# Layer 1's causal mask moved from two TensorE products a pass to one VectorE add; layer 0's compressed results in one bank

## The reference

```python
s_own = jnp.einsum('bhqd,bhkd->bhqk', qc, kown)
m_own = (own + jnp.arange(MOBA_BLOCK))[None, :] <= tpos[:, None]
p = masked_softmax(s_own * HEAD_DIM ** -0.5, m_own)      # masked scores are -inf, their probability is 0
o = jnp.einsum('bhqk,bhkd->bhqd', p, vown)
```

## Time and profile before

| | |
|---|---|
| median of 3 runs | 770.12 us (768.23 to 773.03) |
| the profiled execution | 768.51 us, span 766.7 us |
| PE busy | 745.8 us (97%), 5045 matmuls |
| DVE busy | 497.6 us (65%), 682 instructions |
| ACT busy | 380.4 us (50%), 574 instructions |
| DMA | 146.50 MB, 191 GB/s over the span |
| granted TensorE clock | 9 tenths or more in all 40 slices |

### The profile page before, as it was taken

The page is one execution under the profiler, slowest core; times in us unless marked ns, Lnnn a source line. Parts: engine busy times, 40 slices in busy tenths (PEclk is TensorE's granted clock), DMA queues, the critical chain, the costliest instruction groups (busy, mean ns, idle before and its releaser), DMA issues.

```text
span 766.7 us, 12234 instructions
## 1 busy us (share of the span) xinstructions
PE 745.8 (97%) x5045; PEld 640.7 (84%) x5045; DVE 497.6 (65%) x682; ACT 380.4 (50%) x574; POOL 25.6 (3%) x43
## 2 busy tenths in 40 slices
PE   5999998999999999999999999999999999999998
PEld 3677885468888868788999999999878999999886
DVE  1476759647756755885779999747863745545431
ACT  2554566646354656454553354598443544444330
POOL 3100000100000000012000000000000000000000
PEclk9999999999999999999999999999999999999999
DMA  9994546933367353353746555423444554454611
GB/s 368 406 379 143 200 165 248 390 160 138 110 220 274 110 220 138 138 176 110 274 167 218 168 183 201 167 82 115 160 172 157 220 221 171 159 221 167 217 56 55
DMA packets 21958, 146.50 MB, mean 191 GB/s; under 512 B 2588, under 2 KB 2716, under 8 KB 5392
## 3 DMA queue, kind: packets, MB, share of 16 engines
q1 hardware_dynamic: 20880, 142.62, 50.0%
q0 software_dynamic: 752, 2.06, 0.8%
q10 hardware_dynamic: 272, 1.05, 0.3%
HBM read 144.68 MB, written 1.05 MB: 190 GB/s over the span
## 4 chain that ended last, share of the span: by engine, by line
PE 78%; DVE 3%; issue 2%; ACT 1%; POOL 0%; POOLq 0%; DVEq 0%; ACTq 0%
PE banks L455 22%; PE banks L457 22%; PE banks L456 22%; PE banks L543 3%; PE banks L631 2%; DVE WL L1678 1%; PE banks L567 1%; PE banks L670 1%; PE banks L638 1%; PE banks L923 0%; PE banks L599 0%; PE banks L908 0%; PE banks L674 0%; DVE KT L1710 0%; PE banks L664 0%
## 5 line engine op out<-in xcount | busy, mean ns | idle before, releaser
L1678 DVE TENSOR_TENSOR WL<-RAW,WH 128x2048 fp32r<-128x2048 f32 (+1 forms) x104 | 236.0, 2279 | 63.8 <-ACT WH L1170 63.4
L1170 ACT ACTIVATE WH<-RAW 128x2048 fp32r<-128x2048 f32 (+1 forms) x104 | 197.6, 1906 | 79.0 <-PE banks L457 65.7
L455 PE MATMUL banks<-HH,WH 128*128 128x256 f32 x768 | 217.9, 284 | 0.0
L456 PE MATMUL banks<-HL,WH 128*128 128x256 f32 x768 | 217.3, 283 | 0.0
L457 PE MATMUL banks<-HH,WL 128*128 128x256 f32 x768 | 217.3, 283 | 0.0
L456 PEld LDWEIGHTS banks<-HL,WH 128*128 128x128 f32 x768 | 147.4, 192 | 0.1
L455 PEld LDWEIGHTS banks<-HH,WH 128*128 128x128 f32 x768 | 147.3, 192 | 0.1
L457 PEld LDWEIGHTS banks<-HH,WL 128*128 128x128 f32 x768 | 147.3, 192 | 0.0
L455 PE MATMUL banks<-WH,HH 128*128 128x512 f32 (+1 forms) x320 | 127.1, 397 | 3.5 <-DVE HL L1737 1.9
L457 PE MATMUL banks<-WH,HL 128*128 128x512 f32 (+1 forms) x320 | 124.3, 389 | 0.0
L456 PE MATMUL banks<-WL,HH 128*128 128x512 f32 (+1 forms) x320 | 124.1, 388 | 0.0
(11 more groups left out here) (292 smaller groups left out, 906.1 us busy)
## 6 DMA issues: line engine op xcount, KB each, us to landing
RAW<-in_weights_dram SPq DMA_DIRECT2D x114, 1024.0 KB, 4.8
BIG<-in_weights_dram SPq DMA_DIRECT2D x6, 1024.0 KB, 4.9
ROTS<-in_weights_dram SPq DMA_DIRECT2D x4, 1024.0 KB, 7.0
PROBS<-in_weights_dram SPq DMA_DIRECT2D x2, 1024.0 KB, 12.0
RAW<-in_weights_dram SPq DMA_DIRECT2D x2, 816.0 KB, 9.9
GATE<-in_weights_dram SPq DMA_DIRECT2D x3, 512.0 KB, 9.9
X<-in_x_dram ACTq DMA_DIRECT2D x1, 1024.0 KB, 6.2
QT<-in_weights_dram SPq DMA_DIRECT2D x1, 1024.0 KB, 13.7
```

The costliest lines, as they stand in the source:

```text
L455: pe.matmul(out_, lhsT=w[0], rhs=x[0], start=start, stop=False, **more)
L456: pe.matmul(out_, lhsT=w[0], rhs=x[1], start=False, stop=False, **more)
L1170: do(act.activation(WH[:, home[n], 0:kb * width], RAW[:, slot[n] % RAW_RING, 0:kb * width], ACT.Copy), high_done)
L1678: do(dve.tensor_tensor(WL[:, home[n], w], RAW[:, slot[n] % RAW_RING, w], WH[:, home[n], w], ALU.subtract), low_done)
```

## The change

TensorE leaves the two mask products out in layer 1 (`by_vector`: every pass from layer 1's first), and the last score product marks the bank full. VectorE's `peaks` then adds the mask to the two diagonal blocks of both heads, in place in the two score banks, and waits for that before its minima. In layer 0, kc2 and vc2 go to one bank, columns 0 to 29 and 128 to 255, opened and drained once. The turns of qb (and of q1_1 in layer 1) take "out" banks. The compressed scores are issued at the end of step 3, behind the turns of the probabilities (`last`), and the conditioning row of step 4 behind the weighing (`after`). On VectorE `lows(13)` moves from step 3, ahead of the compressed mask, to the head of step 4's list; on ScalarE the eviction of cmpT moves ahead of `highs(16)` and the gate of zb.1.

On TensorE:

```diff
+        def by_vector(p):
+            return p >= spans[1][0]
...
-            def head_turn(name, t):
+            def head_turn(name, t, kind="turn"):
                 i = rot_index[(name, t)]
-                turn(f"{name}.{t}.T", [QR[:, i % 2, j * P:(j + 1) * P] for j in range(4)], [(roped, i + 1)])
+                turn(f"{name}.{t}.T", [QR[:, i % 2, j * P:(j + 1) * P] for j in range(4)], [(roped, i + 1)], kind)
...
-                        pe.matmul(out_, lhsT=half_of(q, QT, q // 2, t * P, (t + 1) * P),
-                                  rhs=half_of(q, KT, kb, 0, (t + 1) * P), start=(t == 0), stop=False)
+                        mm = pe.matmul(out_, lhsT=half_of(q, QT, q // 2, t * P, (t + 1) * P),
+                                       rhs=half_of(q, KT, kb, 0, (t + 1) * P), start=(t == 0), stop=(by_vector(p) and t == 1))
+                        if by_vector(p) and t == 1:
+                            ps.fill(mm, f"s.{u}")
+                if by_vector(p):
+                    return
...
-            def attention(layer, extra, after={}):
+            def attention(layer, extra, after={}, last={}):
...
                         probs_turn(i - 1)
+                    for what in last.get(i - a, ()):
+                        what()
...
-                ps.fill(mm, "kc2")
                 pe.wait_ge(hid_done, 3)
-                bank = ps.open(pe, "proj", "vc2")
                 for g in range(2):
                     for hb in range(2):
-                        mm = pe.matmul(bank[:, g * HD:(g + 1) * HD],
+                        mm = pe.matmul(bank[:, P + g * HD:P + (g + 1) * HD],
...
-                ps.fill(mm, "vc2")
+                ps.fill(mm, "kc2")
...
-                ps.wait_drained(pe, "vc2")
                 turn("cmpT", [CP[:, t, 4 * g:4 * g + 4, :].rearrange("p h c -> p (h c)")
...
-            attention(0, {0: [lambda: by_tokens("qb", 0), lambda: by_features("za", 0)], 1: [lambda: by_tokens("qb", 1), lambda: head_turn("qb", 0)],
-                          2: [lambda: by_features("za", 1), lambda: head_turn("qb", 1), compress_out],
-                          3: [lambda: by_features("zb", 0)], 4: [lambda: conditioning_row(0, 4)],
+            attention(0, {0: [lambda: by_tokens("qb", 0), lambda: by_features("za", 0)], 1: [lambda: by_tokens("qb", 1), lambda: head_turn("qb", 0, "out")],
+                          2: [lambda: by_features("za", 1), lambda: head_turn("qb", 1, "out"), compress_out],
+                          3: [lambda: by_features("zb", 0)],
...
-                      {3: [compressed_scores]})
+                      {4: [lambda: conditioning_row(0, 4)]}, {3: [compressed_scores]})
...
-                          1: [lambda: head_turn("q1_1", 0), lambda: by_tokens("k1_1", 0),
-                              lambda: head_turn("q1_1", 1)],
+                          1: [lambda: head_turn("q1_1", 0, "out"), lambda: by_tokens("k1_1", 0),
+                              lambda: head_turn("q1_1", 1, "out")],
```

On ScalarE:

```diff
-                evict("kc2", KCT[:, :, :], lambda bank: bank[:, 0:2 * NC].rearrange("p (g c) -> p g c", g=2))
-                evict("vc2", VCM[:, :, :], lambda bank: bank[:, 0:P].rearrange("p (g d) -> p g d", g=2))
+                bank = ps.wait_filled(act, "kc2")
+                do(act.activation(KCT[:, :, :], bank[:, 0:2 * NC].rearrange("p (g c) -> p g c", g=2), ACT.Copy))
+                ps.drain(act.activation(VCM[:, :, :], bank[:, P:2 * P].rearrange("p (g d) -> p g d", g=2), ACT.Copy), "kc2")
...
-                          5: [lambda: highs(16), lambda: gate_half("zb.1", 3), lambda: evict("cmpT", CPT[:, :, :], flat2)],
+                          5: [lambda: evict("cmpT", CPT[:, :, :], flat2), lambda: highs(16), lambda: gate_half("zb.1", 3)],
```

On VectorE, in `peaks` and in layer 0's list:

```diff
+                if by_vector(p):
+                    diagonal = both_scores[:, :, 0:TRI].rearrange("p u (b c) -> p u b c", b=3)[:, :, 0:3:2, :]
+                    mask = const("maskw")[:, 0:P].unsqueeze(1).unsqueeze(1).to_broadcast([P, 2, 2, P])
+                    do(dve.tensor_tensor(diagonal, diagonal, mask, ALU.add))
+                    do.after()
...
-                          3: [lambda: gate(1), lambda: lows(13), compressed_mask],
-                          4: [lambda: gate(2), lambda: row_in(0, 4), compressed_probs, lambda: lows(14)],
+                          3: [lambda: gate(1), compressed_mask],
+                          4: [lambda: lows(13), lambda: gate(2), lambda: row_in(0, 4), compressed_probs, lambda: lows(14)],
```

## The result

The kernel after ran in 764.22 us, median of 6 runs (762.69 to 767.05), the kernel before beside it in 771.46 (768.23 to 773.03): ratio 0.9925 [0.9902, 0.9948]. (The ratios are worked out over the runs of both kernels and are not the quotients of the two medians, here 0.9906.) That is within the 1% that the prediction called no change. A second set of 6 runs gave 764.27 us, with the kernel before at 770.06, and 0.9928 [0.9904, 0.9952]. Two runs of all that were made, one of before and one of a variant, took 1055 and 1215 us at clocks of 0.66 and 0.56 and stand in no comparison.

A forecast was written before the change was run, and what follows sets the result against it. TensorE was taken to bound the kernel, busy 745.8 of 766.7 us. Gains of 2.5 (layer 0), 2.7 (masks) and 0.5 (q1_1's turns) sum to 5.7 us, from 770.12 to 764.4, range 760.0 to 768.8.

The forecast's parts named there:

- Layer 0: Layer 0's attention: turns of pass 5 start at 134.9, 2.5 us ahead; between 0.75 and 4.3.
- The five stops: TensorE's waits in layer 0's attention at 91.28, 101.37, 117.04, 120.61 and 132.52, worth 4.3 us together.
- 1.8 of the 4.3: Layer 0: 1.8 of 4.3 us of removed TensorE stops become a new wait around gate_rows and pass 5's turns.
- VectorE is not late: Layer 0: TensorE keeps all 4.3 us and masks may give 3.4; 8.2 us in all, 761.9; chance 0.16.
- the wait only changes its name: Layer 0: zb.0's copy or cmpT's delayed weight copy holds VectorE; 0.75 us there, 3.3 in all, 766.8; chance 0.21.
- The masks: Layer 1: removing two mask products in 8 passes saves 0.34 us each, 2.7 us; between 1.8 and 3.4.
- q1_1's turns: Layer 1: turns of q1_1 in the "out" banks free the stop at 251.26, worth 0.5 us.
- The cover: Layer 1: probabilities turned 3.9 us after normalising, so VectorE's add costs nothing; without it 3.2 us would be lost.
- rival 3: Layer 1: in-bank add makes VectorE the bound, from about 4 us an add; at 6 us, 780 us; chance 0.03.
- The sum: Whole kernel: 2.5 + 2.7 + 0.5 = 5.7 us; 768.51 becomes 762.8, or 764.4 against the median 770.12.

The follow-up runs named there:

- layer 0 alone: Kernel after with layer 1's mask again two products a pass and q1_1's turns back in the turn banks: 767.80 us, ratio 0.9957.
- the add three times: Kernel after with the mask added three times in each pass of layer 1 on VectorE: 768.98 us, ratio 0.9976.

## Why the prediction was right, and where it was not

**Layer 0, forecast 2.5, measured 2.77: right, by its mechanism.** The five stops went, and VectorE's block of 19.5 us, started by the compressed scores, decided. I had it from 112.85 to 132.35; it ran from 112.32 to 131.82, and the turns began at 134.32 in place of 134.9. The difference of 0.5 is the start, as the whole stretch was 0.3 us ahead. The two stops that appeared, where one was forecast (0.29 and 1.19, together 1.5), are the "1.8 of the 4.3" that the prediction turned into a new wait. That VectorE's order held the rest back was shown by taking the splits out: 1.41 more came, of 1.5. The rival "VectorE is not late" is refuted by that, and "the wait only changes its name" by 2.77 against its 0.75: the copy of the zb.0 bank and the copy behind cmpT were both in time. The split that moved was worth 1.9 to 2.0 of the 2.77; the shared bank, the banks of qb's turns, the moved conditioning row and the moved scores had no runs of their own.

**The masks, forecast 2.7, measured 2.16: right mechanism, wrong size.** The step that failed is "From L638 to the next product is 0.34 us ... I take 0.34". The distance from one product to the next belongs partly to the change of kind behind the fp32 scores, which stays when the products go. I had the right figure in the same rows, 0.23 apart for two like products, and called it the low end. One pass is followed by an fp32 row, and there the whole 0.43 of the earlier trace rows came; at the six passes followed by an fp32r product it is 0.34 less the 0.1 that the next one now takes longer, 0.24; in step 1, where transposes follow, the product behind them came 0.28 sooner (1.27 us after the scores in place of 1.55). That is 0.43 + 0.28 + 6 x 0.24 = 2.15, against 2.16 measured.

**q1_1's turns, forecast 0.5, 0.6 left for them.** Right, as far as a remainder can tell: no run had them alone, and the step that they stand in became 0.58 us shorter at that place (1.33 to 0.75).

**The cover, forecast nothing "at 0.72, nor at 2.29": wrong at 2.29.** The add cost nothing at 0.73. But the step "TensorE turned those probabilities at 250.41, 3.9 us later. The other steps have no less" looked at one reader of VectorE only. The sentence before it names the turns of q and k among what is queued behind; their slack was not worked out. It was 0.95 and 0.89 us in steps 2 and 3 of the kernel before, and 0.35 and 0.33 after the add. An add of 2.2 us cost 4.74, and one of 5.8 us cost 35.8, where the rival had 780 us in all for 6 us an add and the kernel took 799.9. By that slack rival 3 decides from about 1.1 us an add, not from 4. Its 0.03 rested on the wrong margin: the short add kept it from happening (0.73, as the nearest row had it), not 3.9 us of slack.

**The sum, forecast 5.7, measured 5.7 between two executions of equal clock** (766.7 and 761.0; 768.51 and 762.83 us, where 762.8 was forecast). That it fits to the tenth is luck. Two errors cancelled in it: masks 0.5 too high, layer 0 and the rest 0.5 too low. That the median came within 0.2 us is partly luck too: the kernel before, in the same set of runs, had a median of 771.46, 1.3 above the three shown at first, so that the two medians lie 7.2 us apart and not 5.7 (5.8 in the second set), and executions of after that lose 1.5 us by the clock were not in the working.

## What to carry to other kernels

When work moves to an engine that "has time", work out the slack of every reader of that engine behind it, in program order, and take the smallest. Here the last one had 3.9 us and the first 0.35. Price a product that is removed by the distance between two like products, not by that to a neighbour of another kind; where its neighbours change, a run that issues it twice tells its price. And when a stop turns into a wait on a full engine, look at what in that engine's queue has no reader yet: two splits moved by one step each gave back 1.4 us of 1.5.

## What the runs showed of the hardware

The distance from one product to the next depended on what stood in front. A 512-column fp32r product had its successor 0.33 us later when it came straight behind the fp32 scores (277.83 to 278.16), and 0.23 us later when two mask products stood in between (281.68 to 281.91). A 256-column mask product took 0.23 us in the first place and 0.11 to 0.12 in the next ones.

An add of 128x512 on VectorE, in place in two score banks, has a length of 0.70 us and its successor starts 0.73 us after it; the add that only reads a bank has a length of 0.68.

TensorE's granted clock fell from 1.00 to 0.50, the lower of its two levels, for about 3 us in some executions of the same program and not in others. It did so between 164 and 170 us in four of the fourteen profiled executions. TensorE had been busy throughout; its last products were sixteen of two columns (from 160.85 in after), the weighing and the turns. In the first execution of after the six turns there and the first product behind them began 1.20 us apart (164.13 and 165.33), and 0.63 in the second, and the stretch to layer 1 took 1.6 us more. That the two-column products have a part in the fall is not shown.

Two of the profiled executions, of layer 0 alone and of the add three times, had a lower clock early on, 0.85 and 0.77 on average between 30 and 36 us, together with stops of 2.4 and 2.0 us for a conditioning load.
